# Output projection: two row pairs by seven block products instead of one

## What is computed

```python
def rmsnorm(x, g):
    y = xf * lax.rsqrt(jnp.mean(xf * xf, axis=-1, keepdims=True) + EPS)
    return y * g
...
    o = jnp.concatenate([out_a, out_b, out_c], axis=-1) @ w_out
    y = x + rmsnorm(o, g_post)
```

## Time and profile before

| | |
|---|---|
| time, median of 3 runs | 377.34 us (376.68 to 377.36) |
| the profiled execution | 376.8 us, its span 375.1 us |
| granted PE clock, mean over the span | 0.997 |
| PE busy | 367.5 us (98%) |
| DVE busy | 288.4 us (77%) |
| ACT busy | 214.5 us (57%) |
| POOL busy | 143.5 us (38%) |

### The profile page before, as it was taken

How to read it: one execution, slowest core, us unless ns; L and a number is a source line. 1 busy time by engine, 2 the same in 40 slices (tenths; PEclk the granted TensorE clock), 3 DMA queues, 4 the chain that set the end, 5 groups by cost and what they waited for, 6 DMA issues and landing times.

```text
span 375.1 us, 5745 instructions
## 1 busy us (share of the span) xinstructions
PE 367.5 (98%) x2274; PEld 349.2 (93%) x2274; DVE 288.4 (77%) x362; ACT 214.5 (57%) x371; POOL 143.5 (38%) x86
## 2 busy tenths in 40 slices
PE   8999999999999999999999999999999999999994
PEld 7999889999999999999999899999998899988883
DVE  4998897523669977868757999697499999379586
ACT  6986836953652653674959815953948254323622
POOL 3031771572554322843193065311551785002300
PEclk9999999999999999999999999999999999999998
DMA  7995035611130143424210101703213033030632
GB/s 280 396 406 230 0 111 117 224 58 56 58 110 3 56 121 88 142 67 144 72 58 13 45 1 58 280 6 131 90 30 140 2 112 114 0 117 10 217 114 113
DMA packets 18939, 41.14 MB, mean 110 GB/s; under 512 B 4408, under 2 KB 8800, under 8 KB 18656
## 3 DMA queue, kind: packets, MB, share of 16 engines
q1 hardware_dynamic: 18768, 40.70, 31.8%
q10 hardware_dynamic: 144, 0.08, 0.1%
HBM read 35.90 MB, written 4.87 MB: 109 GB/s over the span
## 4 chain that ended last, share of the span: by engine, by line
PE 74%; DVE 11%; DMA 7%; ACT 3%; issue 1%; POOL 1%; SPq 1%; DVEq 0%; POOLq 0%
PE ps L486 39%; PE ps L755 12%; PE ps L773 6%; PE ps L794 4%; DMA mixT<-in_xT 3%; DVE probs L1416 3%; DMA q_rows<-zT 2%; DVE rstdB L1440 2%; DMA spread<-q_rows 1%; PE ps L623 1%; PE ps L699 1%; PE ps L591 1%; DVE zT L1430 1%; PE ps L593 1%; PE ps L612 1%
## 5 line engine op out<-in xcount | busy, mean ns | idle before, releaser
L486 PE MATMUL ps<-x_hi,w_hi 128*128 128x344 f32 x450 | 145.5, 323 | 0.0
L486 PE MATMUL ps<-x_hi,w_lo 128*128 128x344 f32 x450 | 143.7, 319 | 0.0
L486 PE MATMUL ps<-x_lo,w_hi 128*128 128x344 f32 x450 | 143.7, 319 | 0.0
L486 PEld LDWEIGHTS ps<-x_hi,w_hi 128*128 128x128 f32 x450 | 84.6, 188 | 0.4 <-DVE x_lo L1412 0.3
L486 PEld LDWEIGHTS ps<-x_lo,w_hi 128*128 128x128 f32 x450 | 84.5, 188 | 0.2
L486 PEld LDWEIGHTS ps<-x_hi,w_lo 128*128 128x128 f32 x450 | 84.5, 188 | 0.0
L1231 POOL TENSOR_TENSOR w_lo<-w_stage,w_hi 128x1024 fp32r<-128x1024 f32 x17 | 43.4, 2555 | 98.7 <-ACT w_hi L843 84.3
L1373 DVE TENSOR_TENSOR zT<-ps,rstdB 128x344 f32<-128x344 f32 x33 | 16.7, 510 | 19.9 <-PE ps L486 19.8
L843 ACT ACTIVATE w_hi<-w_stage 128x1024 fp32r<-128x1024 f32 x17 | 17.8, 1052 | 20.7 <-PE ps L486 20.7
L1339 POOL TENSOR_TENSOR zT<-zT,x_ring 128x1024 f32<-128x1024 f32 x4 | 12.8, 3202 | 39.0 <-DVE zT L1806 39.0
L755 PE MATMUL ps<-x_hi,w_hi 128*128 128x512 f32 x64 | 25.5, 398 | 0.0
(11 more groups left out here) (346 smaller groups left out, 833.0 us busy)
## 6 DMA issues: line engine op xcount, KB each, us to landing
w_stage<-in_w_tiles SPq DMA_DIRECT2D x17, 512.0 KB, 4.0
mixT<-in_xT SPq DMA_DIRECT2D x8, 516.0 KB, 8.9
x_ring<-in_x_all SPq DMA_DIRECT2D x6, 512.0 KB, 4.6
o_y<-zT SPq DMA_DIRECT2D x5, 512.0 KB, 2.9
zT<-in_w_mem SPq DMA_DIRECT2D x4, 512.0 KB, 11.9
cache<-in_kc SPq DMA_DIRECT2D x8, 256.0 KB, 3.4
...
```

The lines of the kernel that those rows point to most:

```text
L486: last = pe.matmul(ps[:, bank, 0:GN], w[:, slot, wk], xx[:, k, cols], start=(x == 0 and n == 0), stop=(x == KT - 1 and n == 2))
```

## The change

Rows 256 to 511 (blocks 2 and 3), which were two plain blocks, become a second row pair. PE now runs project(0), project(1), the feature groups, seven products for blocks 2 and 3 (a11, s2, s1, s3, a22, s4, a12, with the ones matmul behind s2), and seven for blocks 4 and 5 (the same names with b). The weight sums serve both pairs. Five forms of the second pair use the buffers of the first, so their high parts and sums wait for the product that reads the old content. Blocks 2 and 3 are closed by DVE: `add_to` brings the products together, `scale_half` multiplies with `g_post`, ACT takes the squares (`pair_stats`), and `close_rows` multiplies with the reciprocal root and adds the input. POOL's last two splits and last two input additions are gone. SP's feature transfers now stand ahead of the stores of blocks 3 and 2. The computation for blocks 4 and 5 behind the forms is as before, with higher counts; the last product is still in two column parts.

```diff
-NPLAIN = 4
+NPLAIN = 2
-FORM = {"a22": 0, "a12": 1, "s1": 2, "a11": 3, "s2": 4, "s3": 5, "s4": 6}
-PRODUCT = {"a11": 0, "s2": 1, "s1": 2, "s3": 3, "a22": 4, "s4": 5, "a12": 6}
-PROD_BANK = (5, 6, 7, 3, 4, 2, 0)
+FORM = {"a11": 0, "s2": 1, "s1": 2, "s3": 3, "a22": 4, "s4": 5, "a12": 6,
+        "a22b": 7, "a12b": 8, "a11b": 9, "s1b": 10, "s2b": 11, "s3b": 12, "s4b": 13}
+PRODUCT = {form: n for n, form in enumerate(("a11", "s2", "s1", "s3", "a22", "s4", "a12",
+                                             "a11b", "s2b", "s1b", "s3b", "a22b", "s4b", "a12b"))}
+PROD_BANK = (5, 6, 7, 3, 4, 2, 0) * 2
...
+        RAW_ORDER = ("s3", "s1", "s2", "s4", "s1b", "s3b", "s2b", "s4b")
...
-                if c == 1:
-                    sp.wait_ge(f_done, KT)
-                    sp.dma_start(x_f, d["xT"][:, :, F0:TT]).then_inc(xf_in, 16)
-                if c == 2:
-                    sp.wait_ge(yf_ready, 1)
-                    sp.dma_start(d["o_yT"], y_f).then_inc(side_stored, 16)
-            sp.wait_ge(y5_done, 2)
+            sp.wait_ge(f_done, KT)
+            sp.dma_start(x_f, d["xT"][:, :, F0:TT]).then_inc(xf_in, 16)
+            sp.wait_ge(yf_ready, 1)
+            sp.dma_start(d["o_yT"], y_f).then_inc(side_stored, 16)
+            for n, c in enumerate((3, 2)):
+                sp.wait_ge(y5_done, 2 * n + 2)
+                store_y(c)
+                load_x(c + 2, 1 - c % 2)
+            sp.wait_ge(y5_done, 6)
...
-                    if c == 2 and x == 3:
-                        pe.wait_ge(const_set, 10)
-                        pe.wait_ge(fsum_done, KT - 1)
-                        pe.wait_ge(f_out, KT)
-                        pe.matmul(ps[:, F_BANKS[0], 0:FN], ones[:, :], sum_f, start=True, stop=True).then_inc(f_done, 1)
                 last.then_inc(y_done, 1)
...
-            for c in range(1, NPLAIN):
-                if c > 1:
-                    pe.wait_ge(y_used, c - 1)
-                project(c, (c + 1) % 2)
-                if c == 1:
-                    pe.wait_ge(z_used, 3 * N_TILES)
-                    pe.wait_ge(oflo_done, 2)
-                    for n in range(KT):
-                        project_features(n)
+            project(1, 0)
+            pe.wait_ge(z_used, 3 * N_TILES)
+            pe.wait_ge(oflo_done, 2)
+            for n in range(KT):
+                project_features(n)
...
+            pe.wait_ge(f_out, 6)
             pair_product("a11", block_of(wo_hi, 0, left), block_of(wo_lo, 0, left))
             pe.wait_ge(tlo_done, 2)
+            pe.wait_ge(f_out, KT)
             pair_product("s2", t_high(2), t_low(2))
+            pe.wait_ge(const_set, 10)
+            pe.wait_ge(fsum_done, KT - 1)
+            pe.matmul(ps[:, F_BANKS[0], 0:FN], ones[:, :], sum_f, start=True, stop=True).then_inc(f_done, 1)
             pe.wait_ge(tlo_done, 4)
             pair_product("s1", t_high(1), t_low(1))
-            pe.wait_ge(y_used, 3)
+            pe.wait_ge(y_used, 1)
             pe.wait_ge(tlo_done, 6)
...
             pe.wait_ge(froot_done, 1)
             pair_product("s4", block_of(wo_hi, 1, right), block_of(wo_lo, 1, right))
-            pe.wait_ge(y_used, 4)
-            pe.wait_ge(flo_done, NPROD)
-            f = FORM["a12"]
+            pe.wait_ge(y_used, 2)
+            pair_product("a12", block_of(wo_hi, 1, left), block_of(wo_lo, 1, left))
+
+            pe.wait_ge(snap_done, 1)
+            pair_product("a11b", block_of(wo_hi, 0, left), block_of(wo_lo, 0, left))
+            pe.wait_ge(cadd_done, 1)
+            pair_product("s2b", t_high(2), t_low(2))
+            pe.wait_ge(cadd_done, 4)
+            pair_product("s1b", t_high(1), t_low(1))
+            pair_product("s3b", t_high(3), t_low(3))
+            pe.wait_ge(cadd_done, 5)
+            pair_product("a22b", t_high(4), t_low(4))
+            pe.wait_ge(cadd_done, 6)
+            pair_product("s4b", block_of(wo_hi, 1, right), block_of(wo_lo, 1, right))
+            pe.wait_ge(cadd_done, 7)
+            f = FORM["a12b"]
...
-            next_split(1)
+            form_high("a11")
             y_stats(1, 0)
-            next_split(2)
             features_out(0)
             act.wait_ge(wlo_done, N_TILES)
             t_highs(2, 0, 5)
             t_highs(2, 1, 6)
+            form_high("s2")
+            form_high("s1")
             features_out(1)
             act.wait_ge(scan_done, 6)
             act.wait_ge(gar_done, 3)
+            form_high("s3")
             t_highs(1, 0, 8)
             features_out(2)
             t_highs(1, 1, 8)
+            form_high("a22")
+            act.wait_ge(gate_done, 18)
+            form_high("s4")
+            form_high("a12")
             for n in range(3, KT):
                 features_out(n)
-            act.wait_ge(gate_done, 18)
-            form_high("a22")
-            form_high("a12")
-            form_high("s1")
+            t_highs(3, 0, 8)
+            t_highs(3, 1, 8)
+            act.wait_ge(prod_done, 1)
+            act.activation(u1, blocks(ps[:, PROD_BANK[0], :]), ACT.Copy).then_inc(snap_done, 1)
+            t_highs(4, 0, 8)
+            t_highs(4, 1, 8)
...
+            form_high("a11b", PRODUCT["a11"] + 1)
+            form_high("s1b", PRODUCT["s1"] + 1)
+            def pair_stats(c, first, added):
+
+                parts = sl[:, :] if c == 3 else sy[:, 2:4]
+                act.wait_ge(cadd_done, added)
+                part_square(y_of(c, right), 512, parts[:, 0:1])
+                act.wait_ge(ysq_half, first + 1)
+                act.activation(parts[:, 0:1], parts[:, 0:1], ACT.Identity, scale=1.0 / DM, bias=eps[:, :]).then_inc(yms_done, 1)
+                act.wait_ge(cadd_done, added + 1)
+                part_square(y_of(c, left), 512, parts[:, 1:2])
+                act.wait_ge(ysq_half, first + 2)
+                act.wait_ge(yms_done, first // 2 + 1)
+                act.wait_ge(y_used, 2)
+                act.activation(ry[:, 1 - c % 2:2 - c % 2], parts[:, 1:2], ACT.Sqrt, scale=1.0 / DM,
+                               bias=parts[:, 0:1]).then_inc(yroot_done, 1)
+
+            act.wait_ge(fsum_done, KT - 1)
+            pair_stats(3, 0, 4)
+            form_high("s2b")
+            form_high("s3b")
+            form_high("s4b")
+            pair_stats(2, 2, 6)
+            act.wait_ge(prod_done, NPROD + 1)
+            act.wait_ge(y5_done, 4)
             act.activation(u1, blocks(ps[:, PROD_BANK[0], :]), ACT.Copy).then_inc(snap_done, 1)
...
             finish(0, 1, None)
             for j in range(2):
                 t_raw(2, j, 1 + j)
+            dve.wait_ge(first_done, 4)
+            dve.wait_ge(o_done, 1)
+            form_raw("s3", 2)
+            form_raw("s1", 2)
+            dve.wait_ge(y_done, 1)
+            form_raw("s2", 2)
+            dve.wait_ge(gate_done, 18)
+            form_raw("s4", 2)
             finish(1, 0, None)
             for j in range(2):
                 t_raw(4, j, 5 + j)
-            for n in range(1, KT):
-                add_squares(n)
-                if n < 3:
-                    t_lows(2, n - 1, n)
-                elif n < 5:
-                    t_lows(1, n - 3, n)
...
+            form_low("a11")
+            for n, form in enumerate(("s2", "s1", "s3", "a22", "s4", "a12", None)):
+                add_squares(n + 1)
+                if n < 4:
+                    t_lows((2, 1)[n // 2], n % 2, n + 1)
+                if form is not None:
+                    form_low(form)
+            for j in range(2):
+                t_lows(3, j, 5 + j)
+            for j in range(2):
+                t_lows(4, j, 7 + j)
+            dve.wait_ge(snap_done, 1)
+            dve.wait_ge(flo_done, NPROD)
+            add_to(u2, 1, u1)
+            form_low("a22b")
+            form_low("a12b")
+            add_to(u4, 2, u2, 1)
+            form_raw("s1b", 4, PRODUCT["s1"] + 1)
             dve.wait_ge(froot_done, 1)
             own.link(dve.reciprocal(rstd_f, rstd_f))
             dve.wait_ge(f_out, KT)
             own.link(dve.tensor_tensor(y_f, y_f, rstd_f.unsqueeze(1).broadcast_to([P, KT, FN]), ALU.mult))
+            add_to(u3, 3, u2, 1)
+            dve.wait_ge(y_stored[1], 16)
+            add_to(blocks(y_of(3, right)), 2, u3, 3)
+            form_raw("s3b", 4, PRODUCT["s3"] + 1)
+            add_to(blocks(y_of(3, left)), 4, u3, 3)
+            form_raw("s2b", 4, PRODUCT["s2"] + 1)
             dve.wait_ge(xf_in, 16)
             dve.tensor_tensor(y_f, y_f, x_f, ALU.add).then_inc(yf_ready, 1)
-            dve.wait_ge(y_done, 3)
...
-            form_raw("s2", a22, s_raw["s3"], ALU.subtract)
-            finish(2, 1, 16)
-            dve.wait_ge(gate_done, 18)
-            dve.wait_ge(sraw_done, 3)
-            form_raw("s4", a12, s_raw["s2"], ALU.subtract)
-            form_low("s2", s_raw["s2"])
-            form_low("s3", s_raw["s3"])
-            form_low("s4", s_raw["s4"])
-            finish(3, 0, 16)
-            for j in range(2):
-                t_lows(3, j, 5 + j)
...
+
```

(88 more changed lines are left out.)

85 lines of the change are left out of this document (33 added, 52 removed).

## The result

The changed kernel takes 378.70 us (median of 14 runs), the kernel before, run beside it, 376.87: a ratio of 1.0052, 95% interval 1.0038 to 1.0065. That is slower by 0.5%, inside the range, but outside the likeliest case, which was no change. The profiled execution took 378.24 us with a span of 376.5.

A forecast was written before the change was run, and what follows sets the result against it. PE bounds the stage before, DVE's chain after: 2.87 us of saved matmuls return as about 3.0 us standing still plus 0.2 for restarts and hand-overs, so 377.34 + 0.40 = 377.7 us, range 376.6 to 379.0.

The forecast's parts named there:

- the last product: PE's final product, L829: forecast to start at 366.95 against 366.55 before, 0.40 us later.
- the likeliest case: Whole kernel: time within 0.2% (0.75 us) of the kernel before, called the same, chance 0.60.
- this chain: DVE from the end of s1 to forms a11b (12.85 us) and s2b, 16.8 us long, making PE wait.
- the slack of DVE at s1: DVE, free at about 335.6, waits some 0.4 us for s1's end; delays up to that cost nothing.
- The gaps: PE stands still before products a11b and s2b, waiting for DVE's forms: about 2.0 and 1.1 us.
- the restart: PE's extra time when matmuls resume after standing still: taken as 0.10 us, bounds 0 to 0.3.
- rival 2: DVE chain: each vector operation waits for the one ahead to end, adding 1.2 us, 378.9 us; chance 0.13.
- 5.56 us of closing and storing that the change leaves alone: Stretch behind the last matmul, 369.54 to 375.1: claimed unchanged at 5.56 us, only with higher counts.
- rival 3: PE's clock falls in the gaps, two products take twice their time: 5.6 us more, 383.3 us; chance 0.07.

The follow-up runs named there:

- e2: Changed kernel with DVE's addition of the features' input moved behind form s2b, its store one place later in SP's list: 375.92 us, ratio 0.9982.
- e3: Changed kernel with the features' input addition and block 3's closing both behind form s2b, form s3b right behind the closing: 375.06 us, ratio 0.9954.
- f2: Kernel before with 32 already fulfilled waits added on VectorE (DVE), making its list there as long as the changed kernel's: 376.84 us, ratio 1.0005.
- g1: Changed kernel itself, unaltered, run again beside its variants on one chip: 378.30 us, ratio 1.0048 to the kernel before.
- g4: Changed kernel with 24 already fulfilled waits on VectorE (DVE), run beside the unaltered one on one chip: 377.47 us, ratio 1.0025.
- f1: Changed kernel with 24 already fulfilled waits added on VectorE (DVE), where it idles at 35 to 44 us: 377.91 us, ratio 1.0029.
- f4: Changed kernel with 24 already fulfilled waits added on ScalarE (ACT) instead, as a control: 378.40 us, ratio 1.0045.
- e4: Changed kernel with only block 3's closing moved behind form s2b, the features' input addition left in place: 377.99 us, ratio 1.0022.

## Why the prediction was right, and where it was not

**Right: DVE becomes the bound, by this chain.** Forecast: DVE starts at 336.07, a11b's form ready at 348.92, PE back at 348.97. Measured: DVE starts at 336.02, the form ends at 348.16 + 0.68 = 348.84, PE starts at 348.99. Forecast for s2b: ready at 352.88, start at 352.93; measured 352.76 and 352.91. The gaps were put at about 2.0 and 1.1 us and are 1.86 and 0.92; the slack of DVE at s1 was put at 0.4 and is 0.26. e2 and e3 confirm the chain: with the addition of 2.27 us taken out of it s2b started 2.26 earlier, and with the closing of block 3 out as well PE waited for no form.

**Right: the restart.** Taken at 0.10 from the earlier trace rows, bounds 0 to 0.3: the second matmul comes 0.31 behind the first, the third 0.22 behind the second, so 0.09. The longer gaps did not make it dearer at full clock.

**Right: rival 2 fails.** Sum and form at 351.48 and 352.08 stand 0.60 apart at a length of 0.68, as in the earlier trace rows. The rule of the Trainium skill, "VectorE: DVE Perf Modes", "The DRAIN you can't avoid", as the prediction uses it, would have needed 0.68 there, and by the trace it does not hold for these operations. The same paragraph of the page ends by allowing this: an operation that is not held starts earlier.

**Right: the last product.** It starts at 366.91, forecast 366.95, before 366.55.

**Wrong: "5.56 us of closing and storing that the change leaves alone".** This term was mis-sized. In the profiles it is 1.0 us longer, all of it in the landing of the last store; the instruction packet in front of it costs 0.83 to 0.91 us of time on one chip, 0.49 on another. The step that failed is the reading of the diff: instructions added to DVE were counted by their durations alone, and the list they lengthen was not. The Trainium skill, "Runtime: NRT & Kernel Launch", "Instruction fetch mechanics", says that an engine fetches its instructions in blocks through a DMA queue of its own, and that crossing a block's end is mostly hidden. f2 agrees with the second. The changed kernel is an exception: the fetch met the store that ends the program. Two things on the page differ from this case: its block is 16 KiB, while the q14 packets here are 8 KB, and q14 is not one engine's own, since waits on VectorE and waits on ScalarE each moved packets of it.

**Half right: rival 3.** It was given 0.07 and 5.6 us, as two whole products at the lower level. The mechanism is real, and it came in two of the five profiles with the changed kernel's order (the changed kernel's own, g1 and g4 without, f1 and f4 with). What was off is the size: 3.4 us at the lower level, and the second gap takes most of that up, so 0.42 us. The Trainium skill, "TensorE: Matmul & The Clock Gate", "A second HAM failure mode: psum-queue depth-cycling", tells of short idle times between groups of matmuls that send the clock back and forth; f1, f4 and e4 agree in kind.

**In part luck: that the time lies in the range.** The forecast put the change at 0.40 us; measured beside each other, the two kernels are 378.70 - 376.87 = 1.83 apart. The forecast started from 377.34, the median of three runs, where fourteen gave 376.87, and these 0.47 us hid a part of the miss. And the forecast's own uncertainty reached only some 0.6 above 377.7; the room up to 379.0, in which 378.70 lies, had been left for rival 2, which fails.

**What stays open.** On one chip the changed kernel is 378.30 - 376.47 = 1.83 us slower. The forecast's 0.40 and the packet's 0.83 to 0.91 leave 0.5 to 0.6, more if the packet costs 0.49. The clock explains up to 0.42 in the executions in which it falls, but the run at g1's median, which is the profiled one, shows no fall. The rest was not found; the profiles compared with each other leave nothing over (1.4 = 0.36 + 1.0), so it may lie in how the profiled execution of before stands to its median, 0.3 us, or in executions that have no profile. Five of the fourteen runs of the result took 379.3 to 381.5 us, with mean clocks from 0.990 to 0.995; the clock does not set them apart, no later run of the same kernel took as long, and they are not explained.

Why a packet comes at that place of VectorE's list, and why it came 0.3 us behind the start of the 448th instruction in f2 but 2.6 us behind that of the 447th in the changed kernel, was not settled.
